# Second attention: the last value panel behind the query panels, cut in two halves, with new orders of three engines

## The reference, cut to what matters

```
q, k, v = split_qkv(h, w_in)                     # h: 512 x 1024, w_in: 1024 x 1536
s = einsum('bnqhgd,bnkhd->bnhgqk', qb, kw) * (64 ** -0.5)
s = s - slopes * dist                            # ALiBi; outside of the band: -inf
m = maximum(max(s, -1), sink)
p = exp(s - m)
denom = sum(p, -1) + exp(sink - m)
o = einsum('bnhgqk,bnkhd->bnqhgd', p / denom, vw)
return o.reshape(B, T, 1024) @ w_out             # then x = x + this
```

## Time and profile before

| | before |
|---|---|
| median of 3 runs | 2472.57 us (2471.4 to 2475.39) |
| the profiled execution | 2473.79 us, its span 2472.0 us |
| mean granted TensorE clock | 0.993 |
| PE, DVE, ACT, POOL busy | 2419.6, 1697.0, 945.5, 733.6 us |
| second attention (first score tile to the third output panel) | 1967.16 to 2063.10 us of the span |

### The profile page before, as it was taken

One profiled execution on the slowest core, in us unless ns is written; L12 is line 12 of the kernel. 1 busy time (PEld: TensorE's weight loads), 2 busy tenths in 40 slices (PEclk: granted clock), 3 DMA queues, 4 the chain that ended last, 5 costly groups with the idle time before them and its releaser, 6 DMA issues.

```text
span 2472.0 us, 35059 instructions
## 1 busy us (share of the span) xinstructions
PE 2419.6 (98%) x12082; PEld 2066.1 (84%) x12082; DVE 1697.0 (69%) x3258; ACT 945.5 (38%) x1449; POOL 733.6 (30%) x646
## 2 busy tenths in 40 slices
PE   6999999999999999999999999999999989999998
PEld 5887787787888888888888999999999767888886
DVE  4987878887667767677652478888887785444434
ACT  5224842534233333333333333333333574222232
POOL 0000000000026666666674367777641000000000
PEclk9999999999999999999999999999999999999999
DMA  6235813353244444444445799999996212222321
GB/s 272 94 96 178 297 58 129 137 196 145 93 159 147 139 148 142 150 144 148 145 142 177 254 312 366 364 366 364 361 362 239 77 35 68 96 100 93 102 94 68
DMA packets 179147, 436.28 MB, mean 176 GB/s; under 512 B 33392, under 2 KB 82544, under 8 KB 178672
## 3 DMA queue, kind: packets, MB, share of 16 engines
q1 hardware_dynamic: 123984, 331.74, 38.2%
q0 software_dynamic: 34816, 67.41, 7.8%
q10 hardware_dynamic: 20256, 36.06, 3.9%
HBM read 371.48 MB, written 61.01 MB: 175 GB/s over the span
## 4 chain that ended last, share of the span: by engine, by line
PE 86%; DVE 5%; ACT 1%; issue 1%; DVEq 0%; ACTq 0%
PE ps L562 18%; PE ps L564 18%; PE ps L563 17%; PE ps L968 9%; PE ps L967 9%; PE ps L969 9%; PE ps L807 1%; DVE ar L1823 1%; PE ps L773 1%; DVE ar L1885 1%; DVE tiny L1999 1%; PE ps L797 1%; PE ps L898 0%; DVE wlo L1770 0%; PE ps L1018 0%
## 5 line engine op out<-in xcount | busy, mean ns | idle before, releaser
L562 PE MATMUL ps<-a_hi,whi 128*128 128x512 f32 x1928 | 759.4, 394 | 2.9 <-DVE wlo L1770 1.7
L564 PE MATMUL ps<-a_hi,wlo 128*128 128x512 f32 x1928 | 751.2, 390 | 0.0
L563 PE MATMUL ps<-a_lo,whi 128*128 128x512 f32 x1928 | 750.8, 389 | 0.0
L2743 POOL DMA_INDIRECT w_scratch<-ar x384 | 412.4, 1074 | 925.8 <-issue 815.6
L1770 DVE TENSOR_TENSOR wlo<-raw,whi 128x1024 fp32r<-128x1024 f32 x235 | 287.5, 1223 | 275.0 <-ACT whi L1168 210.6
L562 PEld LDWEIGHTS ps<-a_hi,whi 128*128 128x128 f32 x1928 | 362.4, 188 | 83.1 <-issue 5.9
L563 PEld LDWEIGHTS ps<-a_lo,whi 128*128 128x128 f32 x1928 | 362.5, 188 | 76.8 <-issue 2.9
L564 PEld LDWEIGHTS ps<-a_hi,wlo 128*128 128x128 f32 x1928 | 362.2, 188 | 75.9
L967 PE MATMUL ps<-b_hi,whi 128*128 128x384 f32 (+1 forms) x1176 | 401.7, 342 | 0.0
L968 PE MATMUL ps<-b_lo,whi 128*128 128x384 f32 (+1 forms) x1176 | 401.6, 341 | 0.0
L969 PE MATMUL ps<-b_hi,wlo 128*128 128x384 f32 (+1 forms) x1176 | 401.6, 341 | 0.0
(11 more groups left out here) (311 smaller groups left out, 2885.8 us busy)
## 6 DMA issues: line engine op xcount, KB each, us to landing
raw<-panels SPq DMA_DIRECT2D x302, 512.0 KB, 3.3
late<-panels SPq DMA_DIRECT2D x128, 512.0 KB, 3.8
w_scratch<-rstd SPq DMA_DIRECT2D x32, 768.0 KB, 10.7
ar<-w_scratch SPq DMA_DIRECT2D x128, 192.0 KB, 4.8
ar<-gelu_scratch SPq DMA_DIRECT2D x128, 192.0 KB, 5.6
ar<-mod SPq DMA_DIRECT2D x32, 512.0 KB, 5.0
gelu_scratch<-ar ACTq DMA_DIRECT2D x64, 256.0 KB, 2.0
gelu_scratch<-sq ACTq DMA_DIRECT2D x32, 256.0 KB, 2.0
```

The source lines that it names most:

```text
L562: pe.matmul(bank, w_h, hi[:, k, :], start=(k == 0), stop=False)
L563: pe.matmul(bank, w_h, lo[:, k, :], start=False, stop=False)
L564: last = pe.matmul(bank, w_l, hi[:, k, :], start=False, stop=(k == KT - 1))
L2743: nc.gpsimd.indirect_dma_start(experts, bass.IndirectOffsetOnAxis(offs[:, k:k + 1], 0), vals[:, k:k + 1], None)\
```

## The change

`SW_ORDER` puts the second value panel (3) at the last position, 11, behind the query panels, which move up by one:

```
-SW_ORDER = (0, 2, 4, 5, 6, 7, 1, 3, 8, 9, 10, 11)
+SW_ORDER = (0, 2, 4, 5, 6, 7, 1, 8, 9, 10, 11, 3)
```

The scores of pair 4 need all queries, but no longer all panels: PE's wait ahead of them is for 11 panels read instead of 12. Position 11 is computed by a new function in two halves of four tiles, with attention steps between them:

```
+            def last_value_half(half):
+                if half == 0:
+                    pe.wait_ge(lo_ready, SW + 11 + (1 - U))
+                    pe.wait_ge(bank_free, r_of(SW) + 15)
+                for k in range(4 * half, 4 * half + 4):
+                    last = split3(ps[:, SWB[11], :], 3, k, a_hi[:, k, :], a_lo[:, k, :], k == 0, k == KT - 1)
+                if half:
+                    last.then_inc(used, 1)
```

PE's list:

```
             swa_turn(0)
-            turn_v(1, 2)
             swa_scores(2)
             ...
+            swa_scores(3)
             swa_values(0)
-            swa_scores(3)
             swa_turn(3)
             swa_panel(10)
             swa_turn(4)
+            pe.wait_ge(bank_free, r_of(SW) + 15)
+            swa_scores(4)
             swa_values(1)
             swa_turn(5)
-            swa_panel(11)
+            last_value_half(0)
+            swa_scores(5)
             swa_turn(6)
-            pe.wait_ge(bank_free, r_of(SW) + 16)
-            swa_scores(4)
+            last_value_half(1)
             swa_values(2)
             swa_turn(7)
-            swa_scores(5)
-            swa_values(3)
+            turn_v(1, 3)
             swa_scores(6)
             swa_turn(8)
+            swa_values(3)
             swa_turn(9)
             swa_scores(7)
+            swa_turn(10)
             swa_values(4)
-            swa_turn(10)
             swa_turn(11)
-            out_part(0, 0, 2)
+            out_part(0, 0, 4)
+            swa_turn(12)
             swa_values(5)
-            swa_turn(12)
-            out_part(0, 2, 2)
             swa_turn(13)
             out_part(1, 0, 2)
+            swa_turn(14)
             swa_values(6)
-            swa_turn(14)
+            swa_turn(15)
             out_part(1, 2, 1)
-            swa_turn(15)
+            swa_values(7)
             out_part(1, 3, 1)
-            swa_values(7)
             out_part(0, 4, 4)
```

More of the change, by code:

```diff
@@ L1038, in swa_values @@
                 if m == 0:
-                    pe.wait_ge(v2_done, 2)
+                    pe.wait_ge(v2_done, 1)
                 elif m < 3:
@@ L1044, in swa_values @@
                 if m == 3:
-                    pe.wait_ge(bank_free, r_of(SW) + 16)
+                    pe.wait_ge(v2_done, 2)
                 for s in tiles:
@@ L1660, in _ @@
             swa_exp(2)
+            swa_out(0)
+            bias_tiles(5)
             swa_panel_hi(10)
-            swa_out(0)
             swa_exp(3)
+            bias_tiles(6)
+            bias_tiles(7)
             swa_out(1)
             swa_exp(4)
+            swa_out(2)
             swa_exp(5)
             swa_panel_hi(11)
-            swa_out(2)
+            swa_out(3)
             swa_hi(0)
-            swa_out(3)
-            bias_tiles(5)
             swa_exp(6)
+            swa_exp(7)
             swa_out(4)
             swa_panel_hi(12)
[L1675 to L1682, removed]
             swa_exp(8)
             swa_exp(9)
+            swa_out(5)
+            swa_hi(1)
+            swa_out(6)
+            swa_exp(10)
+            swa_out(7)
+            swa_exp(11)
+            swa_hi(2)
+            swa_out(8)
             swa_hi(3)
-            swa_exp(10)
-            swa_out(8)
-            swa_exp(11)
+            hi_next(0, SO, 0)
             swa_out(9)
             swa_exp(12)
+            swa_out(10)
             swa_exp(13)
-            hi_next(0, SO, 0)
             swa_hi(4)
-            swa_out(10)
             swa_exp(14)
+            swa_out(12)
             swa_exp(15)
+            swa_out(13)
+            swa_out(14)
             swa_hi(5)
-            swa_out(12)
-            swa_out(13)
             swa_hi(6)
-            swa_out(14)
             swa_out(15)
@@ L2563, in swa_lo @@
                                   f32(b_hi[:, kt * 4:kt * 4 + 4, at]), ALU.subtract).then_inc(o2, 1)
-            def pair_bias(m):
-                swa_bias(2 * m)
-                swa_bias(2 * m + 1)
             def swa_turned(n):
@@ L2574, in swa_turned @@
                 dve.tensor_copy(p2T[:, to + first:to + 2, :], ps[:, first:2, :]).then_inc(ptc2, 1)
-            def pair_norm(m):
-                swa_norm(2 * m)
-                swa_norm(2 * m + 1)
             query2(2, 4)
@@ L2590, in _ @@
             dve.wait_ge(bias_ready, NH2 // 2)
-            pair_bias(0)
-            value2(1, 7)
+            swa_bias(0)
+            swa_bias(1)
+            query2(4, 7)
+            swa_norm(0)
             swa_panel_lo(9)
-            pair_bias(1)
-            pair_norm(0)
-            query2(4, 8)
-            swa_panel_lo(10)
[L2598 to L2601, removed]
+            swa_bias(2)
+            swa_bias(3)
+            swa_norm(1)
+            query2(5, 8)
+            swa_norm(2)
+            swa_bias(4)
+            swa_panel_lo(10)
+            swa_bias(5)
+            swa_norm(3)
+            swa_norm(4)
+            query2(6, 9)
+            swa_bias(6)
+            swa_norm(5)
             swa_panel_lo(11)
-            pair_norm(2)
+            swa_bias(7)
             swa_lo(0)
-            pair_bias(3)
-            query2(6, 10)
-            residual(4, 4)
+            query2(7, 10)
+            swa_norm(6)
+            swa_norm(7)
+            dve.wait_ge(bias_ready, NH2)
+            swa_bias(8)
+            swa_bias(9)
             swa_panel_lo(12)
+            swa_norm(8)
+            swa_bias(10)
             swa_lo(1)
[L2610 to L2613, removed]
+            swa_bias(11)
+            value2(1, 11)
+            swa_norm(9)
+            swa_norm(10)
+            value2_out(1, 3)
+            swa_bias(12)
+            swa_bias(13)
+            swa_norm(11)
             swa_lo(2)
-            pair_bias(5)
-            pair_norm(4)
             swa_lo(3)
-            pair_bias(6)
-            pair_norm(5)
-            pair_bias(7)
+            swa_bias(14)
+            swa_bias(15)
+            swa_norm(12)
+            swa_turned(11)
+            swa_norm(13)
             swa_lo(4)
-            swa_turned(11)
-            pair_norm(6)
             lo_next(0, SO, 0)
+            swa_norm(14)
+            swa_norm(15)
+            residual(4, 2)
             swa_lo(5)
-            pair_norm(7)
+            residual(6, 1)
             swa_lo(6)
+            residual(7, 1)
             swa_lo(7)
```

## The result

The changed kernel takes 2459.72 us (median of 5 runs, 2459.17 to 2462.38) against 2473.12 us (5 runs, 2471.4 to 2475.39) for the kernel before, run beside it. The ratio is 0.9948, with a 95% interval of 0.9934 to 0.9961: some 13 us, or half a per cent, faster. Forecast were 2461 us, with 2457.5 to 2467 as the range.

The account below looks back on a forecast made before the run. TensorE, busy 98%, bounds the kernel, so only its holes and low clock can be won: 10.6 − 2.7 = 7.9 us idle plus 4.2 of clock, 12.1 us, gives 2460.5 from the 2472.57 median, taken as 2461; range 2457.5 to 2467.

Parts of the forecast that it names:

- The place: Between 1967 and 2063 us, the second attention: all gain or cost arises there and is handed through to the end.
- The cover: Scores 4 to 6, second attention: scores 4 about 9.6 us earlier, half panels laid under the waits; holes 1.03 and 2.38 gone.
- VectorE as pace: From 2012.8 DVE's list is unbroken for 12.2 us; scores 7 may start at 2024.7, a PE hole of 0.85.
- walk: Following the PE, DVE and ACT lists from 1967.16 with the rows' costs; it ends at a gain of 12.9 us.
- The sum of new holes: PE's waits in the second attention: 2.7 us of new holes against 10.6 before, so 7.9 us less idle time.
- The clock: TensorE's lower clock behind the holes of 2.38 and 3.58 us costs 4.2 us, all won if it stays up.
- A: Rival, 23%: the clock falls once or twice in the new holes, costing 1.5 to 4.2 us, so 2462.5 to 2465.
- B: Rival, 5%: small fp32 products run at half clock from the second half panel to the output's first tiles: 10.4 us, 2471.4.
- C: Rival, 10%: DVE is a tenth slower than its rows, holes grow by 2.7 and the clock drops: 2466.7.
- D: Rival, 4%: norms come late behind panel reads at turns 1 to 4, PE stands four times 4.1 us: 2477.
- The thin covers: Output panel 1, turn_v and values 3 with 0.46, 0.45, 0.15 us to spare, costed at nothing; 1 us if missed.

Follow-up runs that it names:

- residual back: The changed kernel with VectorE's four residual tiles back in one piece, ahead of the norm of group 6: 2462.18 us, ratio 0.9956.
- sized filler: The kernel before with unused matmuls sized to the holes: 10 ahead of scores 6, 7 ahead of scores 7, 8 ahead of turn 11: 2468.45 us, ratio 0.9982.
- scores late: The changed kernel with the scores of pairs 4 and 5 behind both halves of the last value panel again: 2465.44 us, ratio 0.9975.
- late lists only: The kernel before with the new order of PE, DVE and ACT only behind the scores of pair 5: 2466.23 us, ratio 0.9973.
- first filler: The kernel before with unused matmuls, 10 ahead of scores 6 and 14 ahead of turn 11: 2471.86 us, ratio 0.9996.
- whole panel: The changed kernel with both halves of the last value panel together, ahead of the scores of pair 5: 2461.32 us, ratio 0.9959.
- cover only: The changed kernel with the old order of PE, DVE and ACT behind the scores of pair 5: 2466.16 us, ratio 0.9978.

## Why the prediction was right

**The place.** The windows said that the stage alone can change; the rest is the same to 0.1 us (408.9 behind it, 395.98 of 396.00 busy).

**The cover.** Scores 4 were put 9.6 us earlier and are 9.8 earlier; the holes of 1.03 and 2.38 are gone as argued. The prediction gave no price to this part by itself. By the experiments it is 5.5 us alone and 6.2 when taken away.

**VectorE as pace.** The prediction walked DVE's list to 2024.7 for scores 7, 57.54 us into the stage, where they start at 57.47; it had PE there 0.85 us earlier, and the hole is 0.57. The three experiments that shift or load DVE's list came out as the same walk gives for them: 85.62 for 85.5, 84.52 for 84.3 to 84.6, 82.39 for 82.4 to 82.6. What it didn't say is the way over ScalarE that a late bias takes in residual back.

**The sum of new holes.** 2.7 forecast, 1.75 measured. This is the term that was mis-sized: 0.85, 0.53, 0.23 and 0.74 became 0.57, 0.45, 0.20 and 0.53, and the two small ones (0.22, 0.11) are not recorded. Part of this is a mixture of two measures. The 10.62 are recorded holes, from the end of one row to the start of the next; the 2.7 came from the walk, which counts from start to start, and ends of rows overlap the next start by up to 0.1 us. Ahead of values 4 turn 10 takes 1.54 us from start to start (2027.38 to 2028.92), where turn 8 ahead of values 3 takes 1.02: 0.52 of waiting, as walked (0.53), though the record calls it 0.45. The walk itself, one measure throughout, gave 12.9 us; choosing 12.1 instead was the poorer choice. In recorded holes the sum is 8.87 + 4.16 = 13.03, the stage's difference of 13.02. One hole was also read wrongly: the 0.31 ahead of L1050 ends with ScalarE's copy not because transposes need its banks but because the values need the copied probabilities; the sum doesn't change by it.

**The clock.** 4.2 us by adding four rows, 4.1 by the sized filler. Taking no fall for the changed kernel was right too, though the rows left it open. Part of the agreement is luck: the price at scores 6 (1.55) did not stand where I counted it, and was paid 15 us later through ScalarE's list. In scores late and late lists only the fall at scores 6 was hidden, whole or nearly. Adding up slow rows gives the cost only if the engine that was slowed is the one waited for.

**The rivals.** A didn't come: 0.57 and 0.45 us within 3 us left the clock at 1.00, as did 1.85 and 2.07 elsewhere. B falls: 14 us without a split product at 1.00 in the changed kernel. The Trainium skill (TensorE: Matmul & The Clock Gate, Part 4: PE-mode transpose) says that the full rate doesn't engage for a transpose, which doesn't count as busy in the same way; these 14 us, transposes among them, speak against it, and no row here shows it. C: a bias group still takes 1.8 us. D: no hole in the first 35.8 us, as the margins said.

**The thin covers.** Turn_v, values 3 and output panel 1, costed at nothing with 0.45, 0.15 and 0.46 us of cover: no hole is recorded ahead of any of them. In the timeline of DVE what they wait for ends at 2019.11, 2023.04 and 2037.84, and they start at 2019.89, 2023.37 and 2038.42: 0.78, 0.33 and 0.58 us.

## What to carry to other kernels

When several in-order engines pass one piece of work round, find which engine has the unbroken list and feed that one early: here a panel of independent matmuls was worth 2.7 us more for being cut so that the next scores could be issued in its middle, and 2.7 us of harmless work in front of that list cost 1.6. Price a move by walking the lists from start to start with the trace's own durations; the stage came within 1 us of that in six of the eight experiments. The first filler missed by 2.4 us, since the walk had not asked where the holes would go and 2 us of the filler were too much; scores late missed by 1.4, since a low clock was charged where another engine was waited for. Keep to one measure: don't set holes that the record shows against holes that a walk gives. A low clock is a cost only where its engine is waited for: fill the holes with unused matmuls to measure it, and size the filler to end before the wait does.

## What the runs showed of the hardware

How long a hole must be to lower TensorE's clock was not one length: with 1.91 us (filler) it fell, with 1.85 (residual back) and 2.07 (whole panel) it stayed at 1.00, with 2.38 to 4.20 it fell each time. The moment of the fall varied too, from 1.4 us before the hole's end (before, at turn 11) to 0.9 us behind it (scores late), and with it what ran at 1.2 GHz: scores 6 took 3.55 us before and 2.88 in scores late, and before, with the same hole of 3.58 us as in cover only, the low clock went on into the values. Why, these runs leave open.

Nor is a long hole needed. Ahead of the first attention the clock of the kernel before fell at 221.6, where the timeline of PE has two groups of eight matmuls of one column each (L729) and, back to 192 us, no hole longer than this one of 0.48 us:

```profile
220.11 1.05 PE L729 MATMUL ps<-sm,sq 128*128 128x1 f32 x8 [0.48 <-ACT sq L1328]
```

So in the second attention it is shown that filling the holes kept the clock up; that holes are all that lowers it is not. The matmuls of 512 columns whose result nobody reads kept it up as useful ones did: in filler sized it is 1.00 from the scores of pair 4 to the output.
